# Head 1's query weights through ring slot 5, and its query ahead of the first row's sum

## The reference, cut to what matters

```python
q = (x @ w_q).reshape(B, S, PEER_HEADS, 2, PEER_HALF)          # 8 heads, 256 columns each
scores = einsum('bshpk,hpnk->bshpn', q, sub_keys)               # 2 x 128 keys per head
s1, i1 = top_k(scores[..., 0, :], 16); s2, i2 = top_k(scores[..., 1, :], 16)
cand = s1[..., :, None] + s2[..., None, :]                      # 256 sums
top_s, top_c = top_k(cand, 16)                                  # 16 experts per token and head
ids = i1[top_c // 16] * 128 + i2[top_c % 16]; gates = softmax(top_s)
ue, ve = u_tab[ids], v_tab[ids]                                 # two rows of 1024 floats each
out = sum over heads and experts of gates * gelu(ue . x) * ve
```

## Time and profile before

| | |
|---|---|
| median of 3 executions | 1439.15 us |
| lowest and highest | 1437.78 and 1439.69 us |
| profiled execution | 1440.05 us, of which the span between first and last instruction is 1438.1 us |
| PE busy in the span | 1126.6 us, 78% |
| DVE, ACT, POOL busy | 1078.6, 936.3, 602.1 us |
| moved by DMA | 586.12 MB, 408 GB/s over the span; 536.90 MB of it by the gathers' queue |
| TensorE clock granted | 0.894 of full speed on average |

### The profile page before, as it was taken

The page is one execution under the profiler, slowest core; times in us unless marked ns, Lnnn a source line. Parts: engine busy times, 40 slices in busy tenths (PEclk is TensorE's granted clock), DMA queues, the critical chain, the costliest instruction groups (busy, mean ns, idle before and its releaser), DMA issues.

```text
span 1438.1 us, 18872 instructions
## 1 busy us (share of the span) xinstructions
PE 1126.6 (78%) x6799; PEld 882.1 (61%) x6799; DVE 1078.6 (75%) x2599; ACT 936.3 (65%) x1611; POOL 602.1 (42%) x533
## 2 busy tenths in 40 slices
PE   9999999997778877687657978877667866776665
PEld 4567777676666667575546547665555655554554
DVE  1488777778778786788757668977888778878857
ACT  2245677678887888766636667666666766667563
POOL 1044444343543444344425434444544444434451
PEclk9999999999999989999868997998879988888688
DMA  9599999999999999999999999999999999999993
GB/s 357 236 379 425 425 425 426 425 426 382 426 426 406 426 426 427 426 427 427 425 428 425 425 425 400 422 423 419 426 427 426 426 427 426 426 427 422 413 406 133
DMA packets 89479, 586.12 MB, mean 408 GB/s; under 512 B 9661, under 2 KB 14949, under 8 KB 21802
## 3 DMA queue, kind: packets, MB, share of 16 engines
q0 software_dynamic: 74128, 536.90, 89.1%
q1 hardware_dynamic: 15258, 48.02, 8.4%
HBM read 582.79 MB, written 2.10 MB: 407 GB/s over the span
## 4 chain that ended last, share of the span: by engine, by line
DMA 40%; PE 35%; DVE 11%; ACT 8%; issue 3%; POOL 3%; SPq 0%; POOLq 0%; DVEq 0%
DMA arena<-in_uv,ids 39%; PE ps L1138 13%; DVE arena L1731 6%; PE ps L824 6%; ACT arena L1357 4%; POOL arena L616 3%; PE ps L957 3%; PE ps L1033 2%; PE ps L644 2%; ACT actv L1352 2%; PE ps L654 2%; PE ps L637 2%; DMA arena<-in_wq 1%; ACT gel L1349 1%; PE ps L718 1%
## 5 line engine op out<-in xcount | busy, mean ns | idle before, releaser
L616 POOL DMA_INDIRECT arena<-in_uv,ids x512 | 589.1, 1151 | 773.5 <-PE ps L1138 659.3
L1138 PE MATMUL ps<-ident,arena 128*128 128x128 f32 x4076 | 605.7, 307 | 288.2 <-ACT arena L1357 281.8
L1138 PEld LDWEIGHTS ps<-ident,arena 128*128 128x128 f32 x4076 | 528.9, 158 | 385.3 <-ACT arena L1357 336.0
L1731 DVE CUSTOM_DVE_ANT_1 arena<-arena 128x1024 f32<-128x1024 f32 x384 | 467.9, 1225 | 196.5 <-DMA arena<-in_uv,ids 191.1
L1357 ACT ACTIVATE arena<-arena,actv 128x1024 f32<-128x1024 f32 x511 | 554.1, 1131 | 0.0
L1349 ACT ACTIVATE gel<-hid 128x2 f32<-128x2 f32 (+1 forms) x256 | 51.9, 203 | 379.5 <-DVE hid L1731 374.7
L1731 DVE CUSTOM_DVE_ANT_0 arena<-arena 128x1024 f32<-128x1024 f32 x128 | 155.6, 1224 | 63.3 <-DMA arena<-in_uv,ids 62.1
L824 PE MATMUL ps<-arena 128*128 128x128 f32 x992 | 125.1, 288 | 4.8 <-DMA arena<-in_wq 4.8
L1352 ACT ACTIVATE actv<-gel,gates 128x1 f32<-128x1 f32 x511 | 122.8, 287 | 8.4
L824 PEld LDWEIGHTS ps<-arena 128*128 128x128 f32 x992 | 123.1, 205 | 5.1 <-DMA arena<-in_wq 5.1
L957 PE MATMUL ps<-arena 128*128 128x384 f32 x192 | 65.9, 486 | 0.0
(11 more groups left out here) (254 smaller groups left out, 1005.0 us busy)
## 6 DMA issues: line engine op xcount, KB each, us to landing
arena<-in_wq SPq DMA_DIRECT2D x12, 1024.0 KB, 9.4
arena<-in_uv,ids POOLq DMA_INDIRECT x517, 5.1
arena<-in_w_out SPq DMA_DIRECT2D x2, 2048.0 KB, 11.1
arena<-in_w_gate SPq DMA_DIRECT2D x1, 4096.0 KB, 16.5
arena<-in_w_out SPq DMA_DIRECT2D x3, 1024.0 KB, 13.4
arena<-in_w_k SPq DMA_DIRECT2D x4, 512.0 KB, 6.4
arena<-in_w_q SPq DMA_DIRECT2D x2, 1024.0 KB, 9.9
arena<-in_w_v SPq DMA_DIRECT2D x2, 1024.0 KB, 9.5
```

What stands on the lines that cost most here:

```text
L616: nc.gpsimd.indirect_dma_start(out=rows[:, c % RING, 0:n], out_offset=None, in_=a["uv"][:, :], in_offset=bass.IndirectOffsetOnAxis(ap=ids[ ...
L1138: i = mm(ps[:, run_bank(r) + k // 4, (k % 4) * P:(k % 4 + 1) * P], rows[:, c % RING, D + k * P:D + (k + 1) * P], ident[:, :], is_transpose ...
L1731: v.tensor_tensor_reduce(out=r, in0=r, in1=x1[t], scale=1.0, scalar=0.0, op0=ALU.mult, op1=ALU.add, accum_out=hid[:, i, c:c + 1]).then_inc ...
```

## The change

Head 1 gets a home of its own, `R`, which is slot 5 of the ring. Its load waits for `out0_done` instead of head 0's query. Head 2's weights now come next into `wq_a`, behind head 0's query, where head 1's stood. In PE's order `query(1)` moves from behind `combine(0, 0)` to in front of it. Since the weights lie in slot 5, the gather of row 5 of unit 0 waits until that query is done.

```diff
-A, G_, H, K, V = range(5)
-UNITS = ([(0, h, A) for h in range(PH - 1)] + [(0, 7, G_)]
+A, G_, H, K, V, R = range(6)
+UNITS = ([(0, h, R if h == 1 else A) for h in range(PH - 1)] + [(0, 7, G_)]
...
-                    (x1T_0, w_k[:, 2048:2560], w_k[:, 3584:4096]), (kT_flat,), (v_flat,)]
+                    (x1T_0, w_k[:, 2048:2560], w_k[:, 3584:4096]), (kT_flat,), (v_flat,),
+                    (ring[:, 5 * 2 * D:6 * 2 * D],)]
...
-        wq_in = [sem(f"wq_in{b}") for b in range(5)]
+        wq_in = [sem(f"wq_in{b}") for b in range(6)]
...
                 elif b == V:
                     sp.wait_ge(av_done, len(BATCHES))
+                elif b == R:
+                    sp.wait_ge(out0_done, 2)
...
                     if u == 0 and c == 0:
                         pool.wait_ge(score_done, 1)
+                    if u == 0 and c == 5:
+                        pool.wait_ge(q_done, Q_NO[1] + 1)
                     if u == 0 and c == 6:
                         pool.wait_ge(gv_halves, 1)
...
+            query(1)
             for u in range(NU):
                 for c in range(TOPK):
                     combine(u, c)
-                    if u == 0 and c == 0:
-                        query(1)
                     if u == 0 and c == 1:
                         pe.wait_ge(subk_in, 16)
                         key_scores(1)
```

## The result

| | median | lowest to highest | executions |
|---|---|---|---|
| before | 1439.12 us | 1437.78 to 1442.44 | 10 |
| changed | 1442.94 us | 1440.27 to 1445.97 | 10 |

The ratio, taken over all executions, is 1.0023, with a 95% interval of 1.0014 to 1.0031: 3.3 us slower (2.0 to 4.5). The two medians alone differ by 3.8 us. The profiled execution took 1442.54 us with a span of 1440.7.

A forecast was written before the change was run, and what follows sets the result against it. The prediction took the kernel to be bound by DMA at 425 to 427 GB/s. A 6.1 us hole less 2.5 us for the load gave +3.6 us on the median of 1439.15: 1442.7 us, range for 8 in 10 1438.8 to 1445.5.

The forecast's parts named there:

- the chances 0.55 and 0.37: Forecast chances that the whole kernel is slower by more than 0.2% (0.55) or the same within that (0.37).
- Part one, the load: Startup: head 1's and head 2's loads both precede the first gather; one 1.05 MB load leaves the full stretch, gaining 2.5 us.
- Part two, the query: Query 1 on PE starts at 89.75, ends at 93.5 us, 0.9 earlier; the first sum ends some 3.6 us later.
- Part three, the hole: POOL's row 5 gather waits for query 1; DMA runs dry from 90.65 to, in effect, 96.7 us: +6.1 us.
- Reaching the end: After unit 0 the delay persists: every row some 3.6 us later, nothing absorbed by the end.
- no second hole: Unit 1's ids at 118 to 121 us let row 16's data arrive before DMA runs dry, worst-case margin 1 us.
- The later hole: DMA's hole at 346 us, from unit 7's query waiting for weights, moves to about 350 with the same width.
- The short hole: Rival: DMA restarts faster, +1.7 us, or PE sets the loop; 1439 to 1442 us, chance 0.22.
- its second, where only PE's pauses count: Second form of that 0.22 rival: PE sets the loop in 108 to 324 us, so only its pauses count, 1 to 3 us.
- a slow stretch: Rival: PE's clock drops after pauses, 2.3 us per stretch, or a second hole opens; 1444 to 1447 us, chance 0.13.
- The faster case: Rival: unit 7's load meets a shorter queue and the 346 us hole shrinks by up to 8 us; 1435 us, chance 0.08.

The follow-up runs named there:

- experiment 3: Kernel before with query 1 ahead of the first sum, row 5's gather waiting for it, head 2's load held until row 3 is summed: +6.3 us, ratio 1.0044.
- slot 7 runs: Changed kernel with head 1's weights in slot 7's free columns and tile 0's squares, so row 7's gather waits, run twice: -1.0 and -0.3 us against before.
- experiment 7: Changed kernel with head 1's weights in slot 7 and the squares, row 7 waiting, query 1 ahead of tile 1's last projection: +0.6 us against before.
- experiment 8: Changed kernel with slot 7 weights, query 1 ahead of tile 1's last projection, DVE's tile 1 statistics and norm one group later: +2.0 us against before.
- experiment 1: Kernel before with only query 1 moved ahead of the first row's sum, no wait in POOL's queue: -0.9 us against before, ratio 0.9994.
- experiment 4: Changed kernel with POOL's wait for query 1 at the gather of row 3 instead of row 5: +9.6 us against before, ratio 1.0067.
- experiment 2: Kernel before with query 1 ahead of the first sum and row 5's gather waiting for it though nothing needs it: +3.9 us against before, ratio 1.0027.

## Why the prediction came out right

**The sign and the size** were right: 1442.7 us forecast, 1442.94 measured; +3.6 us forecast, +3.3 (+2.0 to +4.5) measured. Whether it is slower by more than 0.2% is left open by the interval, 0.14% to 0.31%, about as the chances 0.55 and 0.37 had it.

**Part one, the load.** Both loads went through in front of the first gather, as said. That a load out of the full stretch is worth about 2.5 us is supported by experiment 3 against the changed kernel (3.0 us, the intervals touch), and by the table of bytes, which fits all ten runs only with this term. As a gain at the end it never showed clear of noise, because in each kernel with an early load DMA lost time elsewhere: 1.7 and 1.2 us in the two slot 7 runs, 3.7 and 3.6 us in experiments 7 and 8, where unit 1's ids became the next wait.

**Part two, the query.** POOL, which the query's end releases, started 18.35 us behind the first gather's start (92.67 - 74.32), 18.4 forecast (93.8 - 75.38). The late first sum costs nothing, shown by experiment 1.

**Part three, the hole.** 6.1 us forecast; 2.43 MB less in 40 us is 5.7. In the window 91 to 95 us DMA moved at 37 GB/s. From POOL's start at 92.67 to the gathers' first bytes it took 1.6 us, as forecast. The Trainium skill's first-byte latency of about 1 us on POOL's path (DMA: Bandwidth & Descriptors, Specifications) is shorter than that. From POOL's start to 108 us DMA moved 5.40 MB, for which 12.7 of the 15.3 us would do at full rate; 2.6 us were lost, where the forecast had 2.9. The delay and the slow start that the earlier trace rows gave were the better guide. Experiment 4 showed that the hole's size carries over, and experiment 3 that the missing bytes do, not the length of POOL's wait, which is 11.16 us in experiments 2 and 3 alike.

**Reaching the end.** Margins held: unit 1's ids at t+43.0 (forecast 118 to 121, that is t+42.6 to t+45.6), no second hole (427 GB/s from 108 to 144 us). From there the delay is +2.75 us at row 16, +2.6 at the load for unit 7, +2.7 at its query. It was 3.6 in the forecast, so the sum was 0.9 too large there, of which 0.4 is the hole (6.1 against 5.7). By bytes the changed kernel is 3.2 us behind at t+60 and as much at t+250 (102.75 MB against 105.17, less the load). What makes up the other half microsecond is open. The later hole kept its width, and in these two executions the end was +3.7; the last microsecond comes behind unit 7's query and lies inside the scatter of an execution.

**The rivals.** The short hole (given 0.22) is refuted in its first form by the 5.7 us. Against its second, where only PE's pauses count, speaks experiment 3: +6.3 us (4.5 to 8.2) with PE idle for 3.6 us between t+17 and t+40 and its clock up. PE's pauses did come, 0.18, 0.74 and 0.91 us before the sums, shorter than the 1 to 2 us expected, and the clock stayed at 1.00. Whether a slow stretch was near can't be read from the length of the waits: after single waits of 2.60 us in experiment 2 and 4.67 us in experiment 4 the sums ran slow, with 0.93 and 0.85 between t+17 and t+40, and after 2.71 us in experiment 3 they did not. The faster case, a shorter load in front of unit 7, did not happen: 14.27 us against 14.16.

## What to carry to other kernels

A buffer borrowed from a ring puts its reader's end in front of a queue. What it costs is not the wait of the issuing engine (11.16 us here) but the time that DMA is dry (5.7 us): count the bytes already queued, and add the slow start. Bytes moved out of a full stretch shorten the run only if DMA doesn't run dry elsewhere for it, so look for the next wait in line first; here it was the next unit's ids, which cost 2.1 us of transfer as soon as the first hole was nearly closed and they came 2.4 us late (experiment 7). And a transfer that waits for the same event as the queue may fill part of the hole, so an isolation test of a wait has to hold it apart.

## What the runs showed of the hardware

The restart of a dry gather queue took 1.6 us from POOL's start to the first bytes and cost 2.6 us to what amounts to full rate, against an estimated 2.9 us for the first gather of the kernel before. SP's queue, released by the same query in experiment 2, moved all of its 1.05 MB in the window 91 to 97 us, in which the gathers' queue moved 0.34 MB. A wait of 2.60 us on PE was followed by a granted clock of 0.50 for some 3 us in experiment 2, one of 2.71 us in experiment 3 by none below 1.00.
